# Two hybrid decoder layers on one core: the output projection's operand turned by VectorE and moved inside SBUF, and the SGU gate block ahead of the mLSTM gate block

## The chip, the core and the metric

The kernel runs on one core of a Trainium2 chip. Its engines run side by side, each with a queue of its own worked off in order: TensorE (PE, matmuls and transposes, results in PSUM), VectorE (DVE), ScalarE (ACT), GpSimd (POOL) and SyncE (SP, which here only issues transfers). They wait for one another by semaphores. The metric is the device time in microseconds (us) of the core; less is better.

## The reference

Two layers, 256 positions, width 2048, all in float32. One layer, cut to what matters here:

```
z = x @ w_in                       # attention q,k,v,gate; SGU u,v,gate; mLSTM q,k,v,o,gate
att = dilated_window_attention(...)                       # 512 columns
sgu = gelu(su) * (w_spatial @ layer_norm(gelu(sv)) + b)   # 512 columns
ml  = head_norm(mlstm(...) * sigmoid(mo))                 # 1024 columns, times a gain
mix = concat([att * silu(ag), sgu * silu(sg), ml * silu(mg)])
x   = layer_norm(alpha * x + mix @ w_out)
```

The matmul `mix @ w_out` needs `mix` with its columns on the partitions, that is, turned.

## The kernel before

**Blocks and chunks.** The projections run as 27 blocks of 512 output columns per layer. A block is 8 chunks of 256 input rows (`chunks`, L358). Float32 accuracy comes from splitting both operands into a high and a low part: a chunk is 2 row tiles x 2 position tiles x 3 products, 12 matmuls of 128x512. A chunk's weights are loaded by SyncE into a ring of four (`w_raw`, L324, 512 KB), ScalarE writes the high part (`w_hi`, L736) and VectorE the low part, the residue (`w_lo`, L1060). SyncE loads chunk c when the residue of chunk c - 4 is done; ScalarE overwrites a slot of `w_hi` when TensorE has used the chunk that was in it. All three write their work out by hand, in the order of the program; nothing is reordered.

**The end of a layer.** Blocks 21 and 22 are the second half of the mLSTM gate (`N_MG1`) and the SGU gate (`N_SG`); blocks 23 to 26 are the output projection (`N_OUT`). During block 21 TensorE also does the mLSTM value products, and VectorE the head outputs (`head_output`, L1419). During block 22 VectorE normalises the heads (L1462, `h_norm`), GpSimd multiplies by the head gain (L1732) and by the gate (L1737).

**The turned operand.** `mix` is [128 positions, 2, 2048]. TensorE turns it in 64 pieces, 32 per layer (`transposes`, L391, by a matmul with the identity), four pieces for a chunk of the output projection, into PSUM. ScalarE copies a chunk's high part out (L755) and VectorE the residue (L1084). The first block interleaves these with its chunks (`first_block`, L448), and `OUT_ORDER` puts the SGU columns, ready last, at the end:

```
                chunks(N_SG, Q_SG, 1, 0, 4)
                transposes(mix, CH, OUT_ORDER, 0, ((h_done, (l + 1) * MH), (mix_att, l + 1)))
                transposes(mix, CH, OUT_ORDER, 1)
                chunks(N_SG, Q_SG, 1, 4, CH)
                first_block(N_OUT, Q_OUT, mix, CH, OUT_ORDER, 2, ...
```

GpSimd also loads two rows broadcast over 128 partitions for the LayerNorm, 1 MB each: the gain into `z` (L1729) and the bias into `store` (L1741).

## Time and profile before

| | |
|---|---|
| median of 3 runs | 1271.35 us (1270.79 to 1271.76) |
| span of the profiled execution | 1269.9 us |
| TensorE busy | 1257.0 us (99%) |
| VectorE busy | 893.0 us (70%) |
| ScalarE busy | 705.4 us (56%) |
| GpSimd busy | 244.0 us (19%) |
| queue of SyncE's transfers, share of the 16 DMA engines | 60.6% |

The span runs from the first to the last instruction of one profiled execution; the median is of other executions, without a profile, and stands 1.45 us above it. Busy shares are means over the whole span. A matmul row's end is modelled, so starts of rows and the chain of work are the better clock on TensorE.

### The profile page before, as it was taken

The page shows a single profiled execution, that of the slowest core. Times are in us where ns is not written, and L with a number is a line of the kernel's source. Part 1 is how long each engine was busy: PE and PEld are TensorE (multiplying, and loading weights), DVE is VectorE, ACT ScalarE, POOL GpSimd, SP SyncE. Part 2 cuts the span into 40 slices and gives each one's busy share as a digit, 9 for nine tenths or more (in the row PEclk, how much of TensorE's full clock was granted, in tenths as well). Part 3 has the DMA queues.
Part 4 walks back from the last instruction along what each step waited for, and adds up shares of the span by engine and source line. Part 5 has one row for each costly group of instructions (what it writes and reads, how often), then busy time and mean ns, then how long its engine had stood idle before and what let it go on. Part 6 is the DMA issues. An engine that isn't in the chain of part 4 may idle for free.

```text
span 1269.9 us, 16388 instructions
## 1 busy us (share of the span) xinstructions
PE 1257.0 (99%) x6342; PEld 1040.2 (82%) x6342; DVE 893.0 (70%) x1229; ACT 705.4 (56%) x989; POOL 244.0 (19%) x268
## 2 busy tenths in 40 slices
PE   9999999999999999999999999999999999999996
PEld 8888888878888888888888788888888888888885
DVE  5686876876667655865785779768665776567656
ACT  5477476575555544444563775666755555345441
POOL 0321522522220000400003223334131200004000
PEclk9999999999999999999999999999999999999998
DMA  9968768765665555465657587678546556565562
GB/s 336 310 209 261 236 189 277 260 192 164 204 195 174 184 186 185 152 230 190 207 186 238 183 282 245 193 258 282 184 149 215 183 157 209 165 197 198 186 212 86
DMA packets 129277, 264.97 MB, mean 209 GB/s; under 512 B 8824, under 2 KB 8976, under 8 KB 128688
## 3 DMA queue, kind: packets, MB, share of 16 engines
q1 hardware_dynamic: 123712, 247.23, 60.6%
q0 software_dynamic: 3680, 13.28, 3.0%
q10 hardware_dynamic: 1808, 3.42, 0.7%
q8 instruction: 50, 0.82, 0.3%
q14 instruction: 27, 0.22, 0.0%
HBM read 258.61 MB, written 5.28 MB: 208 GB/s over the span
## 4 chain that ended last, share of the span: by engine, by line
PE 86%; ACT 4%; DVE 4%; POOL 3%; issue 2%; DVEq 0%; POOLq 0%; ACTq 0%
PE ps L373 79%; ACT arena L810 2%; DVE w_lo L1060 2%; ACT w_hi L736 2%; PE ps L444 1%; PE ps L671 1%; PE ps L391 1%; PE ps L639 1%; POOL arena L1684 1%; PE ps L533 0%; POOL arena L1680 0%; PE ps L518 0%; ACT arena L807 0%; PE ps L355 0%; DVE arena L1133 0%
## 5 line engine op out<-in xcount | busy, mean ns | idle before, releaser
L1060 DVE TENSOR_TENSOR w_lo<-w_raw,w_hi 128x1024 fp32r<-128x1024 f32 x408 | 527.1, 1305 | 326.4 <-ACT w_hi L736 324.5
L736 ACT ACTIVATE w_hi<-w_raw 128x1024 fp32r<-128x1024 f32 x408 | 427.3, 1058 | 388.9 <-PE ps L373 339.3
L373 PE MATMUL ps<-w_hi,xT_hi 128*128 128x512 f32 x1616 | 636.2, 394 | 0.7 <-DVE w_lo L1060 0.7
L373 PE MATMUL ps<-w_hi,xT_lo 128*128 128x512 f32 x1616 | 629.6, 390 | 0.0
L373 PE MATMUL ps<-w_lo,xT_hi 128*128 128x512 f32 x1616 | 629.0, 389 | 0.0
L373 PEld LDWEIGHTS ps<-w_hi,xT_hi 128*128 128x128 f32 x1616 | 303.4, 188 | 64.3 <-issue 1.3
L373 PEld LDWEIGHTS ps<-w_hi,xT_lo 128*128 128x128 f32 x1616 | 303.3, 188 | 64.0
L373 PEld LDWEIGHTS ps<-w_lo,xT_hi 128*128 128x128 f32 x1616 | 303.6, 188 | 61.4
L292 POOL TENSOR_TENSOR carried<-ident 1x1 f32<-1x1 f32 x30 | 19.6, 652 | 454.8 <-DVE arena L1416 178.7
L1217 DVE CUSTOM_DVE_ANT_0 mix<-xres,mix 128x1024 f32<-128x1024 f32 x64 | 89.0, 1390 | 1.1
L807 ACT ACTIVATE arena<-arena 32x256 f32<-32x256 f32 x128 | 53.2, 416 | 15.6 <-DVE arena L1137 14.0
L373 PE MATMUL ps<-ahead,xT_hi 128*128 128x512 f32 x160 | 49.8, 392 | 0.0
L1630 POOL TENSOR_TENSOR su<-z,sincos 128x128 f32<-128x128 f32 x24 | 23.6, 1005 | 122.0 <-ACT z L796 100.9
L1404 DVE SCALAR_TENSOR_TENSOR conv_y<-ps,cw,conv_y 128x255 f32<-128x255 f32 (+2 forms) x96 | 41.7, 476 | 1.1
L1060 DVE TENSOR_TENSOR ahead<-w_raw,ahead 128x1024 fp32r<-128x1024 f32 x23 | 27.5, 1223 | 15.1 <-ACT ahead L736 15.0
L736 ACT ACTIVATE ahead<-w_raw 128x1024 fp32r<-128x1024 f32 x23 | 23.8, 1056 | 22.8 <-DMA w_raw<-w_out_dram 7.2
L373 PEld LDWEIGHTS ps<-ahead,xT_hi 128*128 128x128 f32 x160 | 29.7, 188 | 5.9
L373 PE MATMUL ps<-ahead,xT_lo 128*128 128x512 f32 x80 | 31.2, 390 | 0.0
L810 ACT ACTIVATE arena<-arena 32x256 f32<-32x256 f32 x64 | 26.6, 416 | 7.3 <-DVE arena L1133 6.5
L825 ACT ACTIVATE arena<-arena 32x256 f32<-32x256 f32 x64 | 26.6, 415 | 6.8 <-DVE arena L1165 5.9
L967 ACT ACTIVATE arena<-conv_y 128x512 f32<-128x512 f32 x16 | 10.1, 633 | 32.7 <-DVE conv_y L1404 32.7
L1732 POOL TENSOR_TENSOR store<-store,hg 128x1024 f32<-128x1024 f32 x4 | 11.4, 2876 | 76.5 <-DVE store L1462 76.5
(244 smaller groups left out, 825.3 us busy)
## 6 DMA issues: line engine op xcount, KB each, us to landing
w_raw<-w_in_dram SPq DMA_DIRECT2D x367, 512.0 KB, 4.5
w_raw<-w_out_dram SPq DMA_DIRECT2D x64, 512.0 KB, 4.8
mix<-gate_w_dram SPq DMA_DIRECT2D x32, 512.0 KB, 5.6
xres<-x_dram ACTq DMA_DIRECT2D x4, 512.0 KB, 8.4
v_dram<-arena POOLq DMA_DIRECT2D x4, 512.0 KB, 6.3
z<-v_dram POOLq DMA_DIRECT2D x8, 256.0 KB, 5.6
z<-ln_g_dram POOLq DMA_DIRECT2D x2, 1024.0 KB, 7.7
store<-ln_b_dram POOLq DMA_DIRECT2D x2, 1024.0 KB, 7.9
```

Of the source, the lines that this page charges most:

```text
L292: nc.gpsimd.tensor_tensor(carried[0:1, at:at + 1], ident[0:1, 0:1], ident[0:1, 0:1], ALU.mult)
L373: mm = pe.matmul(ps[2 * s + t][:], a[:, order[c] * KC + k, t * P:(t + 1) * P], b[:, k], start=(c + k + i == 0), stop=(c == CH - 1 and k == ...
L391: tr = pe.transpose(ps[4 + u % 4][:, (k * TT + t) * P:(k * TT + t + 1) * P], src[:, t, at * P:(at + 1) * P], ident[:])
L444: mm = pe.matmul(ps[t][:], a[:, c * KC + k, t * P:(t + 1) * P], b[:, k], start=False, stop=(c == CH - 1 and k == KC - 1 and i == 2))
L736: A(hi_of(n, c), w_raw[:, c % RING], ACT.Copy).then_inc(w_hi_done, 1)
L807: mv_ = A(dst.rearrange("p m (r t u i) -> p u t (m r) i", r=RES, t=TT, u=4)[:, u], src.rearrange("p (t f q i) -> p f t q i", t=TT, f=4, i= ...
L810: mv_ = A(dst.rearrange("p m (t u s) -> p u t m s", t=TT, u=4)[:, u], src.rearrange("p (t m f s) -> p f t m s", t=TT, m=PAIRS, f=4)[:, f], ...
L825: e = A(pTC[f * 32:(f + 1) * 32, :, u * 32:(u + 1) * 32], zp[u * 32:(u + 1) * 32].rearrange("p (s f i) -> p f s i", s=SLOTS, f=4)[:, f], A ...
L1060: TTn(lo_of(n, c), w_raw[:, c % RING], hi_of(n, c).bitcast(F32), ALU.subtract).then_inc(w_lo_done, 1)
L1217: f = V.tensor_tensor_reduce(gate_junk, xres[:, tt, half * KH:(half + 1) * KH], gate_rows[buf], 1.0, 0.0, ALU.mult, ALU.add, gate_acc[:, t ...
L1404: f = STT(y, ps[4 + hf][:, t * SEQ:(t + 1) * SEQ - back], cw[:, m, j:j + 1], y, ALU.mult, ALU.add)
L1630: G.tensor_tensor(rope_a[:, :, :, c], v[:, :, :, c], trig(1), ALU.mult)
```

## The change

Per layer:

- Blocks 21 and 22 change places: the SGU gate is now block 21, the second half of the mLSTM gate block 22.
- TensorE's 32 transposes of `mix`, the functions `transposes` and `first_block` and the PSUM copies are gone. `mix` is handled in four parts of 512 columns: attention, SGU, first and second mLSTM half.
- VectorE turns a part in one instruction (`turn_mix`): each 32x32 square in itself, written to `mix_zT`. To reach a full turn the 32-row strips must change partitions: SyncE copies them in 16 transfers a part (`move`), each of 32 partitions x 2 x 128 numbers (32 KB), from `mix_zT` to `mix_T`.
- ScalarE and VectorE then write the high part and the residue of the operand from `mix_T` (`operand`), for the last part in two halves.
- SyncE issues the moves between weight loads: after the load of chunk 0 of block 22 (attention), of chunk 6 (first mLSTM half), of chunk 7 (SGU), and of chunk 7 of block 23 (second mLSTM half). Before each group it waits for the turn.
- GpSimd multiplies the SiLU of the first gate half by its gain early, and only the second half's heads by theirs after `h_norm`. VectorE does the products with the heads. Both halves of the SGU gate's SiLU are done by ScalarE from PSUM.
- The LayerNorm gain is loaded after the attention part's residue (its buffer `z` now holds that part), the bias after the product of the second mLSTM half.
- The output projection takes its chunks in plain order.

```diff
@@ -298,7 +314,17 @@
         @block.sync
         def _(sp):
             for l in range(DEPTH):
-                def load(w, n, col, order, gate=()):
+                def move(p):
+
+                    sp.wait_ge(mix_turned, l * PARTS + TURN_ORDER.index(p) + 1)
+                    src = mix_zT[p].rearrange("p (f t x) -> p f t x", f=4, t=TT)
+                    dst = mix_T[p].rearrange("p (t u x) -> p u t x", t=TT, u=4)
+                    for u in range(4):
+                        for f in range(4):
+                            sp.dma_start(dst[f * QUARTER:(f + 1) * QUARTER, u], src[u * QUARTER:(u + 1) * QUARTER, f]
+                                         ).then_inc(mix_moved[p], 16)
+
+                def load(w, n, col, order, gate=(), moves={}):
 
                     for c in range(CH):
...
+                        if c in moves:
+                            move(moves[c])
 
...
                     load(w_in, n, col * BW, plain)
+                load(w_in, N_MG1, (MG + 1) * BW, plain, moves={0: ATT, 6: ML_A, 7: SGU})
                 for i in range(D // BW):
-                    load(w_out, N_OUT + i, i * BW, OUT_ORDER)
+                    load(w_out, N_OUT + i, i * BW, plain, moves={7: ML_B} if i == 0 else {})
 
...
@@ -692,31 +695,28 @@
                     mm = pe.matmul(ps[o + 1][:, 0:MD + 1], scE[:, h, 2 * P:3 * P], vM[:, 1, h, :],
                                    start=False, stop=True)
                     mm.then_inc(mnum_ps, 1)
-                chunks(N_MG1, Q_MG1, 0, 5, CH)
-
-
-                chunks(N_SG, Q_SG, 1, 0, 4)
-                transposes(mix, CH, OUT_ORDER, 0, ((h_done, (l + 1) * MH), (mix_att, l + 1)))
-                transposes(mix, CH, OUT_ORDER, 1)
-                chunks(N_SG, Q_SG, 1, 4, CH)
-                first_block(N_OUT, Q_OUT, mix, CH, OUT_ORDER, 2, {
-                    2: ((h_done, (l + 1) * MH), (mix_ml, l + 1)),
-                    6: ((z_dve, taken_dve(l, Q_SG)),)})
+                chunks(N_SG, Q_SG, 0, 5, CH)
+
+                chunks(N_MG1, Q_MG1, 1, 0, CH)
+
+                for c in range(CH):
+                    pe.wait_ge(mixT_lo, step(l, c))
+                    chunks(N_OUT, Q_OUT, 0, c, c + 1)
                 for i in range(1, last_out):
-                    chunks(N_OUT + i, Q_OUT + i, i % 2, 0, CH, OUT_ORDER)
+                    chunks(N_OUT + i, Q_OUT + i, i % 2, 0, CH)
 
                 last = (N_OUT + last_out, Q_OUT + last_out, last_out % 2)
-                chunks(*last, 0, CH, OUT_ORDER, tiles=(1,), done=tile1_ps)
+                chunks(*last, 0, CH, tiles=(1,), done=tile1_ps)
                 if l == DEPTH - 1:
-                    chunks(*last, 0, CH, OUT_ORDER, tiles=(0,))
+                    chunks(*last, 0, CH, tiles=(0,))
                 else:
-                    chunks(*last, 0, 3, OUT_ORDER, tiles=(0,))
+                    chunks(*last, 0, 3, tiles=(0,))
                     unit(l + 1, 0)
                     unit(l + 1, 1)
...
-
-                    for u in range(u0, u1):
-                        if u >= c0:
-                            split(n, u, u + 1)
-                        act.wait_ge(xt_ps, mix_first(l) + u + 1)
-                        A(xT_hi[:, order[u] * KC:(order[u] + 1) * KC, :],
-                          ps[4 + u % 4][:].rearrange("p (k t) -> p k t", k=KC), ACT.Copy).then_inc(xt_hi, 1)
+                def operand(p, j=0, n=PART_TILES):
+
+                    act.wait_ge(mix_moved[p], (l + 1) * 16 * 16)
+                    act.wait_ge(w_used, used(l, N_MG1, 2 * p + 1))
+                    A(mix_target(xT_hi, p, j, n), mix_source(p, j, n), ACT.Copy).then_inc(mixT_hi, 1)
 
                 if l == 0:
                     for k in range(KC):
...
                 act.wait_ge(h_done, (l + 1) * MH)
                 A(rstd[:, 0], mv[:, :, :, 1], ACT.Sqrt, bias=eps[:]).then_inc(h_root, 1)
-                split(N_SG, 2, 4)
-                act.wait_ge(w_used, used(l, N_SG, -1))
-                A(mix[:, 0, 3 * BW:4 * BW], ps[0][:], ACT.Silu).then_inc(z_act, 1)
-                act.wait_ge(z_dve, taken_dve(l, Q_MG1))
-                A(mix[:, 1, 3 * BW:4 * BW], mix[:, 1, 3 * BW:4 * BW], ACT.Silu).then_inc(mg_silu, 1)
-                split(N_SG, 4, 8)
-                operand(N_OUT, RING, CH, OUT_ORDER, 0, 2)
-                split(N_OUT, 0, 4)
-                operand(N_OUT, RING, CH, OUT_ORDER, 2, 4)
+                split(N_MG1, 2, 4)
+                act.wait_ge(w_used, used(l, N_MG1, -1))
+                A(mix[:, 0, BW:2 * BW], ps[0][:], ACT.Silu)
+                A(mix[:, 1, BW:2 * BW], ps[1][:], ACT.Silu).then_inc(z_act, 1)
+                split(N_MG1, 4, 6)
+                operand(ATT)
+                split(N_MG1, 6, 8)
+                split(N_OUT, 0, 2)
+                operand(SGU)
+                split(N_OUT, 2, 4)
                 act.wait_ge(w_used, used(l, N_OUT, -1))
-                A(mix[:, 0, BW:2 * BW], ps[2][:], ACT.Silu)
-                A(mix[:, 1, BW:2 * BW], ps[3][:], ACT.Silu).then_inc(z_act, 1)
-                operand(N_OUT, RING, CH, OUT_ORDER, 4, CH)
+                A(mix[:, 0, 3 * BW:4 * BW], ps[2][:], ACT.Silu)
+                A(mix[:, 1, 3 * BW:4 * BW], ps[3][:], ACT.Silu).then_inc(z_act, 1)
+                operand(ML_A)
+                split(N_OUT, 4, 8)
+                operand(ML_B, 0, KC)
+                operand(ML_B, KC, KC)
                 for i in range(1, D // BW):
                     split(N_OUT + i, 0, 8)
 
...
-                        TTn(xT_lo[:, k, :], ps[4 + u % 4][:].rearrange("p (k t) -> p k t", k=KC),
-                            xT_hi[:, k, :].bitcast(F32), ALU.subtract).then_inc(xt_lo, 1)
+                def operand(p, at, j=0, n=PART_TILES):
+
+                    dve.wait_ge(mixT_hi, l * STEPS + at + 1)
+                    TTn(mix_target(xT_lo, p, j, n), mix_source(p, j, n), mix_target(xT_hi, p, j, n).bitcast(F32),
+                        ALU.subtract).then_inc(mixT_lo, 1)
+
+                def turn_mix(p):
+
+                    V.transpose(mix_zT[p].rearrange("p (f b s) -> p b f s", f=4, b=TT * PART_TILES),
+                                mix[:, :, p * BW:(p + 1) * BW]).then_inc(mix_turned, 1)
 
...
@@ -1443,33 +1443,49 @@
                         f = V.bn_aggr(mv[:, t, h, :], stats[:, t, h, :])
                     f.then_inc(h_done, 1)
 
-                split(N_MG1, 0, 4)
-                take(N_MG1, 1, vM[:, 1, 2:4, 0:MD])
-                split(N_MG1, 4, 5)
+                split(N_SG, 0, 4)
+                take(N_SG, 1, vM[:, 1, 2:4, 0:MD])
+                split(N_SG, 4, 5)
+                turn_mix(ATT)
 
                 dve.wait_ge(mo_sigmoid, l + 1)
                 for h in range(3):
-                    split(N_MG1, 5 + h, 6 + h)
+                    split(N_SG, 5 + h, 6 + h)
                     head_output(h)
-                split(N_SG, 0, 1)
+                split(N_MG1, 0, 1)
                 head_output(3)
-                split(N_SG, 1, 3)
+                split(N_MG1, 1, 3)
                 dve.wait_ge(h_root, l + 1)
                 own(V.reciprocal(rstd[:, 1], rstd[:, 0]))
-                for t in range(TT):
-                    for h in range(MH):
+                for h in range(MH):
+                    for t in range(TT):
                         v = store[:, 1 + h // 2, t, (h % 2) * MD:(h % 2 + 1) * MD]
                         f = TS(v, v, mv[:, t, h, 0:1], rstd[:, 1, t, h:h + 1], ALU.subtract, ALU.mult)
                 f.then_inc(h_norm, 1)
-                split(N_SG, 3, 4)
-                take(N_SG, 0, mix[:, 1, 3 * BW:4 * BW])
-                split(N_SG, 4, 8)
-                operand(N_OUT, RING, CH, OUT_ORDER, 0, 2)
-                split(N_OUT, 0, 4)
-                operand(N_OUT, RING, CH, OUT_ORDER, 2, 4)
+                dve.wait_ge(h_norm, l + 1)
+                dve.wait_ge(ml_gain, l + 1)
+                own(TTn(mix[:, :, 2 * BW:3 * BW], mix[:, :, 2 * BW:3 * BW], store[:, 1], ALU.mult))
+                turn_mix(ML_A)
+                split(N_MG1, 3, 4)
                 dve.wait_ge(z_act, taken_act(l, Q_SG))
                 TTn(mix[:, :, BW:2 * BW], mix[:, :, BW:2 * BW], su[:], ALU.mult).then_inc(z_dve, 1)
-                operand(N_OUT, RING, CH, OUT_ORDER, 4, CH)
+                dve.wait_ge(z_dve, taken_dve(l, Q_SG))
+                turn_mix(SGU)
+                split(N_MG1, 4, 6)
+                operand(ATT, 0)
+                split(N_MG1, 6, 8)
+                split(N_OUT, 0, 2)
+                operand(SGU, 1)
+                split(N_OUT, 2, 4)
+                dve.wait_ge(store_gain, l + 1)
+                dve.wait_ge(z_act, taken_act(l, Q_MG1))
+                TTn(mix[:, :, 3 * BW:4 * BW], mix[:, :, 3 * BW:4 * BW], store[:, 2], ALU.mult).then_inc(z_dve, 1)
+                dve.wait_ge(z_dve, taken_dve(l, Q_MG1))
+                turn_mix(ML_B)
+                operand(ML_A, 2)
+                split(N_OUT, 4, 8)
+                operand(ML_B, 3, 0, KC)
+                operand(ML_B, 4, KC, KC)
 
                 def residual(i, t):
...
-                pool.wait_ge(msc_done, (l + 1) * MH)
+                pool.wait_ge(mg_silu, l + 1)
+                for t in range(TT):
+                    v = mix[:, t, 2 * BW:3 * BW]
+                    f = G.tensor_tensor(v, v, hg[:, 0], ALU.mult)
+                f.then_inc(ml_gain, 1)
+
+                pool.wait_ge(h_norm, l + 1)
+                for t in range(TT):
+                    f = G.tensor_tensor(store[:, 2, t, :], store[:, 2, t, :], hg[:, 1], ALU.mult)
+                f.then_inc(store_gain, 1)
+                pool.wait_ge(mixT_lo, l * STEPS + 1)
                 carry_pool()
                 pool.dma_start(ln_gain, row(ln_g, 0, D)).then_inc(ln_gain_landed, 16)
-                pool.wait_ge(h_norm, l + 1)
-                for t in range(TT):
-                    f = G.tensor_tensor(store[:, 1:3, t, :], store[:, 1:3, t, :], hg[:], ALU.mult)
-                own(f)
-                pool.wait_ge(mg_silu, (l + 1) * 2)
-                for t in range(TT):
-                    v = mix[:, t, 2 * BW:4 * BW].rearrange("p (a c) -> p a c", a=2)
-                    f = G.tensor_tensor(v, v, store[:, 1:3, t, :], ALU.mult)
-                f.then_inc(mix_ml, 1)
-                pool.wait_ge(mix_ml, l + 1)
+                pool.wait_ge(z_dve, taken_dve(l, Q_MG1))
                 carry_pool()
                 pool.dma_start(ln_bias, row(ln_b, 0, D)).then_inc(ln_bias_landed, 16)
 
```

SyncE's queue in layer 0, from the last gate-weight loads of the attention part to the start of layer 1, before:

```order
L310 DMA mix<-gate_w_dram 128x1024 x2
L324 DMA w_raw<-w_in_dram 128x2x512 x92
L324 DMA w_raw<-w_out_dram 128x2x512 x32
L324 DMA w_raw<-w_in_dram 128x2x512 x20
L310 DMA mix<-gate_w_dram 128x1024 x2
```

and now:

```order
L350 DMA w_raw<-w_in_dram 128x2x512 x85
L324 DMA z<-arena 32x2x128 x16
L350 DMA w_raw<-w_in_dram 128x2x512 x6
L324 DMA arena<-arena 32x2x128 x16
L350 DMA w_raw<-w_in_dram 128x2x512
L324 DMA arena<-arena 32x2x128 x16
L350 DMA w_raw<-w_out_dram 128x2x512 x8
L324 DMA arena<-arena 32x2x128 x16
L350 DMA w_raw<-w_out_dram 128x2x512 x24
```

The row of 124 loads is cut in four places by 16 small transfers; one load stands alone between the second and the third group.

VectorE's queue from the second and third residue of block 22 on (L1060 is a weight residue, L1084 an operand residue before and a turn now, L1079 an operand residue now), before:

```order
L1060 TENSOR_TENSOR w_lo<-w_raw,w_hi 128x1024 x2
L1458 RECIPROCAL rstd<-rstd 128x8
L1462 TENSOR_SCALAR store<-store,mv,rstd 128x256 x8
L1060 TENSOR_TENSOR w_lo<-w_raw,w_hi 128x1024
L1095 COPY mix<-ps 128x512
L1060 TENSOR_TENSOR w_lo<-w_raw,w_hi 128x1024 x4
L1084 TENSOR_TENSOR xT_lo<-ps,xT_hi 128x512 x2
L1060 TENSOR_TENSOR w_lo<-w_raw,w_hi 128x1024 x4
```

and now:

```order
L1459 RECIPROCAL rstd<-rstd 128x8
L1463 TENSOR_SCALAR store<-store,mv,rstd 128x256 x8
L1467 TENSOR_TENSOR mix<-mix,store 128x2x512
L1084 STREAM_TRANSPOSE arena<-mix 128x8x4x32
L1060 TENSOR_TENSOR w_lo<-w_raw,w_hi 128x1024
L1471 TENSOR_TENSOR mix<-mix,su 128x2x512
L1084 STREAM_TRANSPOSE arena<-mix 128x8x4x32
L1060 TENSOR_TENSOR w_lo<-w_raw,w_hi 128x1024 x2
L1079 TENSOR_TENSOR xT_lo<-z,xT_hi 128x1024
L1060 TENSOR_TENSOR w_lo<-w_raw,w_hi 128x1024 x4
```

A product and a turn have come in front of the residue of chunk 3, and another pair in front of that of chunk 4.

## Rows read from the trace of the kernel before

**Rows 1.** The page, busy time: engine, busy us (share of span), instructions.
```profile
PE 1257.0 (99%) x6342; PEld 1040.2 (82%) x6342; DVE 893.0 (70%) x1229; ACT 705.4 (56%) x989; POOL 244.0 (19%) x268
```

**Rows 2.** List of waits, TensorE: total us, times, longest us.
```profile
PE ps L355 <- POOL ident L1567: 1.6, 1, 1.6
PE ps L373 <- DVE w_lo L1060: 0.7, 1, 0.7
```

**Rows 3.** Chain of waits in order of time: start us, us, what.
```profile
510.41 19.06 PE ps L373 x84
529.47 0.87 PE ps L391 x8
...
541.27 0.87 PE ps L391 x8
...
1158.16 0.87 PE ps L391 x8
```

**Rows 4.** Instructions by line: count, ns min/median/max, first and last start.
```profile
L1133 DVE STREAM_TRANSPOSE arena<-z x4: 1230/1238/1248, 244.9 to 895.8; 128x1024 f32<-128x1024 f32 x4
L1137 DVE STREAM_TRANSPOSE arena<-z x16: 1094/1132/1155, 63.5 to 806.4; 128x512 f32<-128x512 f32 x16
L1060 DVE TENSOR_TENSOR w_lo<-w_raw,w_hi x408: 1176/1225/3499, 15.5 to 1242.2; 128x1024 fp32r<-128x1024 f32 x136
L1084 DVE TENSOR_TENSOR xT_lo<-ps,xT_hi x16: 672/681/685, 535.7 to 1185.5; 128x512 fp32r<-128x512 f32 x16
L736 ACT ACTIVATE w_hi<-w_raw x408: 1037/1060/1112, 14.4 to 1241.2; 128x1024 fp32r<-128x1024 f32 x136
L755 ACT ACTIVATE xT_hi<-ps x16: 577/582/621, 530.5 to 1184.2; 128x512 fp32r<-128x512 f32 x16
```

**Rows 5.** Timeline of VectorE: start us, us, line, count, [idle before]; merged rows include gaps.
```profile
497.32 2.36 DVE L1060 TENSOR_TENSOR w_lo<-w_raw,w_hi 128x1024 fp32r<-128x1024 f32 x2 [2.83 <-ACT w_hi L736]
...
517.05 1.23 DVE L1060 TENSOR_TENSOR w_lo<-w_raw,w_hi 128x1024 fp32r<-128x1024 f32 x1 [1.49 <-ACT w_hi L736]
...
518.42 2.67 DVE L1462 TENSOR_SCALAR store<-store,mv,rstd 128x256 f32<-128x256 f32 x8
...
524.48 3.50 DVE L1060 TENSOR_TENSOR w_lo<-w_raw,w_hi 128x1024 fp32r<-128x1024 f32 x1 [1.65 <-ACT w_hi L736]
...
524.48 11.30 DVE L1060 TENSOR_TENSOR w_lo<-w_raw,w_hi 128x1024 fp32r<-128x1024 f32 x4 [1.65 <-ACT w_hi L736]
```

**Rows 6.** Timelines of GpSimd and ScalarE in block 22, same columns.
```profile
524.49 2.40 POOL L1732 TENSOR_TENSOR store<-store,hg 128x1024 f32<-128x1024 f32 x1
...
521.05 0.60 ACT L986 ACTIVATE mix<-ps 128x512 f32<-128x512 f32 x1
```

**Rows 7.** SyncE's issues: by line (ns min/median/max), and timeline (start us, us, count).
```profile
L324 SPq DMA_DIRECT2D w_raw<-w_out_dram x20: 367/368/368, 528.0 to 579.2; - x20
...
L320 SPq DMA_DIRECT2D mix<-x_t_dram x7: 358/469/537, 1.8 to 13.1; - x7
...
0.81 0.86 SPq L315 DMA_DIRECT2D w_raw<-w_in_dram  x2
...
528.01 0.37 SPq L324 DMA_DIRECT2D w_raw<-w_out_dram  x1
```

**Rows 8.** Transfers: issuing queue, count, KB each, median us from issue to landing.
```profile
w_raw<-w_in_dram SPq DMA_DIRECT2D x367, 512.0 KB, 4.5
w_raw<-w_out_dram SPq DMA_DIRECT2D x64, 512.0 KB, 4.8
...
store<-ln_b_dram POOLq DMA_DIRECT2D x2, 1024.0 KB, 7.9
out_dram<-xres SPq DMA_DIRECT2D x4, 512.0 KB, 2.7
```

**Rows 9.** Stretches at the end: us, busy by engine, granted clock, DMA share, GB/s.
```profile
1258.00:1260.00 2.00, 1.83 (x9) 1.18 (x7) 0.13 (x1) 0.00 (x0) 0.00 (x0) 1.00 0.13 51
...
1262.00:1264.00 2.00, 0.00 (x0) 0.00 (x0) 2.00 (x3) 0.00 (x0) 0.00 (x0) 0.70 0.00 0
```

72 lines of the change are left out of this document (30 added, 42 removed).

## The prediction, made before the changed kernel ran

> **What bounds the kernel now.** I read the busy table first: TensorE is busy 1257.0 us, 99% of the span of 1269.9 [rows 1]. The list of waits says the same from the other side: after the 1.6 us at the very start, the longest wait of a matmul on another engine is 0.7 us [rows 2]. So every microsecond taken from TensorE's instruction stream is a microsecond of the kernel, as long as nothing else arrives late; and each new late arrival is paid in full. Next I read the chain of work around the output projection of layer 0 [rows 3]. It is matmuls without a break: seven chunks in 19.06 us, so 2.72 us for a chunk (12 matmuls), then pieces of transposes between the chunks.
>
> That gives the clock face for the rest. Call the two gate blocks A (block 21) and B (block 22), and a block's chunks A0 to A7. From 510.41 on stand A5, A6, A7 and B0 to B3 [rows 3]; so B0 starts at 518.6, B3 at 526.8 and B4 at 529.5. Layer 1 shows the same picture 628.7 us later (the transposes of 529.47 are there at 1158.16 [rows 3]).
>
> **What is removed.** Eight transposes take 0.87 us of the chain [rows 3], 0.109 us each. There are 32 per layer, which makes 3.5 us, and 7.0 us in both layers. All of it is on the path. With no transposes, B4 to B7 would run from 529.5 to 540.4 and the first chunk of the output projection, O0, would start at 540.4.
>
> **What is added on VectorE, and when.** Per layer: four turns of 128x1024, two products of 128x1024, and residues of the operand in five instructions from SBUF instead of eight from PSUM. The nearest row for a turn is the one with whole runs, 1.24 us [rows 4]; the strided form took 1.13 for half the size, 2.26 for a full one [rows 4]. The new turn writes runs of 32, so I take 1.24 and keep 2.26 as the far end. A residue of 128x1024 takes 1.22, and a product of that size is priced the same [rows 4]. The operand's residues nearly cancel (eight of 0.68 [rows 4] against 4 x 1.22), so 4 x 1.24 + 2 x 1.22 = 7.4 us per layer are new. VectorE isn't the bound, so this sum doesn't matter; its place does.
>
> The attention turn stands in block A after A4's residue. VectorE does A4 and A5 there from 497.3 to 499.7 [rows 5], and TensorE reaches A5 only at 510.4: hidden, priced at nothing. If that cover were gone it would cost its 1.24 us.
>
> In block B it is tight. VectorE ends B2's residue at 518.2 and the eight normalising instructions at 521.1 [rows 5]. Before, B3's residue came next. Now a product and a turn come first: 521.1 + 1.22 + 1.24 = 523.6. GpSimd multiplies by the head gain from that same moment; in the trace its 128x1024 product takes 2.40 us [rows 6], and VectorE's residue that starts beside it takes 3.50 instead of 1.22 [rows 5], that is, it waits until GpSimd is through. The changed kernel has only 128x512 there, half of 2.40; so I add 1.2 us (0 at the good end): the turn ends at 524.75. B3 follows at 526, before 526.8. Then product, turn, B4: 526 + 1.22 + 1.24 + 1.22 = 529.7 against 529.5, a stall of 0.2 at most here. On the credit side four large GpSimd products, which now stretch four residues to 11.3 us [rows 5], are gone. The other edits there (the loop order of the normalising, a copy of 0.68 us off VectorE, a SiLU more on ScalarE in its place) stay under a microsecond on engines that then wait for TensorE; the two small gain products that GpSimd now does in the mLSTM part cost VectorE 1.2 us each at most, where a residue has some 6 us to spare. ScalarE has its SiLU output at 521.7, and 0.6 later the second [rows 6], in time for the second product.
>
> **What is added on SyncE, the term that decides.** Each part is carried by 16 transfers of 32 KB, all issued by SyncE, which also issues every weight load, in order. The moves stand behind the loads of B0 (attention), B6 (first mLSTM half), B7 (SGU) and O7 (second mLSTM half). What waits for them is the load written next: B1, B7, O0 and O8 (the next block's first). Issuing a load takes 0.367 us of the queue, and never less around the output projection [rows 7]; two issues in a row at the start took 0.86 us, 0.43 each, and seven issues in the crowded start took 0.47 in the median and up to 0.54 [rows 7]. No row shows a 32 KB copy inside SBUF being issued. I take 0.42, near the pitch of the two in a row; the ends are 0.37 (nothing between issues) and 0.54. Below the lower end I see no row, but rival 1 asks what it would bring.
>
> B1: held until about 499.8 + 16 x 0.42 = 506.5, lands 4.5 us later [rows 8], at 511; ScalarE can't take it before A5 is used, at 513.1. Hidden.
>
> B7: SyncE waits for the turn at 524.75, then 16 x 0.42 = 6.7 us: issued at 531.5, landed at 536.0, and with ScalarE's 1.06 and VectorE's 1.22 [rows 4] plus 0.1 between them ready at 538.4. TensorE wants it at 537.6: 0.8 late.
>
> O0: one load and 16 more issues, 7.1 us: issued at 538.6. In the kernel before it was issued at 528.0 [rows 7]. It lands after 4.8 us [rows 8] and is split 2.4 us later: 545.8. TensorE is free for it at 540.4. **A stall of 5.4 us** (with B7's part in it). The following loads go out at once behind it and don't stall again.
>
> Second mLSTM half: counted from O0's start, VectorE does O1, the SGU residue, O2 and O3, the product and the turn, six steps of about 1.2, so the turn ends at +7.2. The last of 16 issues starts at +13.5. For the landing I have 2.7 us (SBUF to DRAM, idle) as a lower end and 4.5 (a weight load) as an upper one [rows 8]; I take 3.4, between the two, since the bias row of the LayerNorm, 1 MB, is loaded beside it and takes 7.9 us [rows 8]. Then 0.58 + 0.68 [rows 4] for half a part: +18.2. TensorE wants it for O6 at 6 x 2.72 = +16.4: **a stall of 1.8 us.** The load of O8, issued at +13.9, is ready at +21.1, and TensorE wants it at 16.4 + 1.8 + 5.4 = +23.6: hidden.
>
> The GpSimd loads move too: the LayerNorm gain, 1 MB, is now fetched after the attention residue, about 533, beside the SGU moves, where before it was fetched in the mLSTM part. I price it inside the 4.8.
>
> **The sum.** Per layer -3.5 + 5.4 + 1.8 = +3.7; two layers +7.4. The profiled execution spans 1269.9 us, and the median of the runs is 1271.35, that is 1.45 above the span; the same 1.45 is kept: 1269.9 + 7.4 + 1.45 = 1278.8 us, 0.6% slower.
>
> **Weighed against the Trainium skill.** An issue costs SyncE at least 0.36 to 0.37 us whether the transfer has 256 or 512 KB [rows 7]. DMA: Bandwidth & Descriptors (Rules for kernel authors) says to coalesce many small transfers because under 64 KB one pays mostly overhead; that speaks against 128 transfers of 32 KB. The same page (Issuing engines are not separate DMA queues) says that the time on the issuing sequencer is usually small beside the transfer; if so, the pitch would hardly count and the full gain would show, 1264.3. By the trace it isn't small here. Its fit for one transfer (2.0 us plus bytes at 436 GB/s; Anatomy of one DMA), given for GpSimd's path, would make an estimate of 2.1 us for the landing of the last move instead of 3.4, and the sum 2.6 us smaller; no row here shows that.
>
> **Rivals.**
> 1. The queue holds nothing up; faster. The stalls shrink by 33 pitches and by 16 pitches. With 0.26 us or less the first is gone (5.4 - 33 x 0.16), the second too, and the whole 7.0 us show: 1264.3. Even balance is at 49 x (0.42 - p) = 3.7, so p = 0.345. Below that pitch the kernel is faster. For it: the issue row may hold work that grows with the load's 256 rows. Against: the first two loads, of half the size, took 0.43 each all the same [rows 7].
> 2. Gain and stall cancel. Pitch 0.37, no collision with GpSimd, a landing of 4.0: O0 stalls 5.4 - 1.65 - 1.2 - 0.8 = 1.8, the second half 1.8 - 0.8 - 0.7 = 0.3. Net -1.4 per layer: 1268.5, at the edge of no change; with only two of the three, about 1271.
> 3. The queue is worse than thought. Pitch 0.54 as under load: O0 stalls 5.4 + 4.0, the second half 1.8 + 1.9 + 1.1 with a landing of 4.5; net +10.7 per layer: 1292.8. The pieces of 512 bytes, and the 1 MB rows beside them, could do that.
> 4. The clock. TensorE's granted clock is 1.00 (2.4 GHz) while it works; its last matmul ends at about 1259.8, and over 1262 to 1264 the mean is 0.70 [rows 9], so the clock has fallen to the lower level (0.5, 1.2 GHz) some 3 us after the stop. A stall of 5.4 us is long enough for that. At half speed the first chunks of O take up to 2.7 us longer, of which the second stall hides 1.8, since its chain doesn't pass through TensorE: 0.9 per layer, 1280.6. It goes with the forecast and stays inside its width.
> 5. The turns are slow (2.26 us): two turns stand before B4, so up to 2 us more at O0 and 1 at the second half: +6, 1284.8.
>
> **How the numbers follow.** Forecast with 4 and 5 around it: 0.50. Rival 3: 0.15. Rival 2: 0.15. Rival 1, in full or between 1264 and 1268.8: 0.20. A measurement of this kernel can tell about 0.2%, 2.5 us, from no change. Slower by more: 0.50 + 0.15 = 0.65. Within: 0.15. Faster: 0.20. The range reaches from inside rival 1 to rival 3's end: 1266 to 1292.
>
> **What would show it.** In the profile of the changed kernel: (a) the 64 transposes of the mix are gone and each chunk of O0 to O7 follows the last without a gap of 0.44 us; (b) SyncE's queue shows four bursts of 16 issues per layer, each 6 to 9 us; (c) ScalarE waits on the DMA of w_out for O0, and TensorE on the residue of that chunk, about 5 us, in both layers; (d) a second, shorter wait of TensorE at O6, put down to the operand's residue; (e) no wait in block A. What would make it wrong: bursts under 5 us, or O0's load issued before 533. If TensorE waits already at B4, the turn or the collision with GpSimd was mis-sized and not the queue.

## The result, and the profile of the changed kernel

| | before | changed |
|---|---|---|
| median of four runs | 1271.55 us | 1301.0 us |
| profiled execution, its span | 1269.9 us | 1300.9 us |
| TensorE busy, share of the span | 1257.0 us, 99% | 1264.3 us, 97% |

The changed kernel takes 1.0229 of the time before (95% interval 1.0215 to 1.0244): 2.3% slower, 29.5 us. The prediction said slower, by 0.6%, 1278.8 us with a range of 1266 to 1292. The sign held; the time lies 9 us above the range.

The page's busy row of the changed kernel stands against [rows 1]; its waits of TensorE (total us, times, longest) stand against [rows 2], where the longest was 0.7 us behind the start.

```profile
PE 1264.3 (97%) x6278; PEld 1041.6 (80%) x6278; DVE 897.5 (69%) x1233; ACT 705.0 (54%) x983; POOL 236.0 (18%) x268
```

```profile
PE ps L402 <- DVE w_lo L1060: 20.5, 9, 5.0
PE ps L402 <- DVE xT_lo L1079: 4.2, 2, 2.2
PE ps L384 <- POOL ident L1583: 1.6, 1, 1.6
```

TensorE now waits for split weights (w_lo) and for the operand of the output projection (xT_lo). Its busy time has grown by 7.3 us although 7.0 us of transposes are gone: some of its matmuls ran slower.

SyncE's timeline of layer 0 (start us, length us, line, transfer, count) shows the four bursts of moves (L324) and the loads (L350) between them:

```profile
499.79 11.39 SPq L324 DMA_DIRECT2D z<-arena  x16
511.22 9.15 SPq L350 DMA_DIRECT2D w_raw<-w_in_dram  x6
525.37 10.18 SPq L324 DMA_DIRECT2D arena<-arena  x16
535.59 0.58 SPq L350 DMA_DIRECT2D w_raw<-w_in_dram  x1
536.22 10.49 SPq L324 DMA_DIRECT2D arena<-arena  x16
546.76 11.67 SPq L350 DMA_DIRECT2D w_raw<-w_out_dram  x8
560.48 10.45 SPq L324 DMA_DIRECT2D arena<-arena  x16
```

A burst takes 10.2 to 11.4 us, that is 0.64 to 0.71 us for an issue. B7's load goes out at 535.59, O0's at 546.76, where it was 528.01 before [rows 7]. ScalarE, which splits the weights first, waits for just these two, and already for B1's load, held up by the attention burst (its timeline, idle time before the row in brackets):

```profile
515.09 1.06 ACT L736 ACTIVATE w_hi<-w_raw 128x1024 fp32r<-128x1024 f32 x1 [4.77 <-DMA w_raw<-w_in_dram]
...
541.49 1.06 ACT L736 ACTIVATE w_hi<-w_raw 128x1024 fp32r<-128x1024 f32 x1 [13.54 <-DMA w_raw<-w_in_dram]
550.99 1.06 ACT L736 ACTIVATE w_hi<-w_raw 128x1024 fp32r<-128x1024 f32 x1 [8.45 <-DMA w_raw<-w_out_dram]
...
572.20 1.15 ACT L752 ACTIVATE xT_hi<-arena 128x512 fp32r<-128x512 f32 x2 [4.87 <-DMA arena<-arena]
```

And TensorE, in its own timeline:

```profile
527.64 0.50 PE L402 MATMUL ps<-w_hi,xT_hi 128*128 128x512 f32 x1 [0.84 <-DVE w_lo L1060]
...
543.86 0.79 PE L402 MATMUL ps<-w_hi,xT_hi 128*128 128x512 f32 x1 [4.25 <-DVE w_lo L1060]
...
553.46 0.76 PE L402 MATMUL ps<-w_hi,xT_hi 128*128 128x512 f32 x1 [4.11 <-DVE w_lo L1060]
...
573.60 0.59 PE L402 MATMUL ps<-w_hi,xT_hi 128*128 128x512 f32 x1 [1.99 <-DVE xT_lo L1079]
...
1197.16 0.76 PE L402 MATMUL ps<-w_hi,xT_hi 128*128 128x512 f32 x1 [5.01 <-DVE w_lo L1060]
...
1218.14 0.50 PE L402 MATMUL ps<-w_hi,xT_hi 128*128 128x512 f32 x1 [2.16 <-DVE xT_lo L1079]
```

These are the first matmuls of B3, B7, O0 and O6 in layer 0, and of O0 and O6 in layer 1. The stretches between them show the granted clock (columns: stretch, its length, TensorE's busy time and matmuls, clock, DMA share, GB/s):

```profile
540.00:543.80 3.80, 0.00 (x0) 0.92 0.51 158
543.80:549.20 5.40, 5.34 (x12) 0.50 0.32 79
...
553.40:557.00 3.60, 3.54 (x9) 0.53 0.79 278
557.00:570.00 13.00, 13.00 (x59) 1.00 0.76 226
...
573.60:577.00 3.40, 3.40 (x9) 0.54 0.99 348
```

After each of the three long waits of layer 0 TensorE works at the lower level (0.5, 1.2 GHz): the twelve matmuls of B7 take 5.3 us, where a chunk takes 2.72 at full clock [rows 3].

**The balance of a layer.** O0 starts at 553.46 and not at 540.4: 13.1 us. From O0 to O6 it takes 20.1 us in place of 16.3: 3.8. After O6 nine matmuls stand 0.43 apart and not 0.23: 1.8. Less 3.5 for the transposes, that is 15.2; the chain of work in layer 1 begins its end 14.9 us later than before (1124.18, 1109.24 before). In layer 1 O0 is late by 13.1 again (1197.16, where 540.4 + 628.7 + 14.9 is 1184.0), but from O0 to O6 it takes 21.0 us, 4.7 too many, behind a burst of 11.2 us, and after O6 seven slow matmuls cost 1.4: less 3.5, 15.7. Together that is 30.9; the spans differ by 31.0. The waits of 0.84 and 0.51 us before B3 and B4 add nothing: they lie before O0, inside its 13.1.

### The profile page after: what moved, and what is told of

Its sections match the earlier page's. It is cut to its first block, busy times and chain, and to the rows that moved or that the text cites. A ratio compares the mean times of both kernels' runs of the same rounds, so it can differ in the third digit from the quotient of the medians.

```text
span 1300.9 us, 16392 instructions
## 1 busy us (share of the span) xinstructions
PE 1264.3 (97%) x6278; PEld 1041.6 (80%) x6278; DVE 897.5 (69%) x1233; ACT 705.0 (54%) x983; POOL 236.0 (18%) x268
## 4 chain that ended last, share of the span: by engine, by line
PE 79%; SPq 6%; DVE 5%; ACT 3%; issue 2%; DMA 2%; POOL 2%; DVEq 0%; POOLq 0%; ACTq 0%
PE ps L402 73%; SPq L324 6%; DVE w_lo L1060 2%; PE ps L458 1%; ACT w_hi L736 1%; PE ps L674 1%; DMA w_raw<-w_out_dram 1%; DMA w_raw<-w_in_dram 1%; DVE arena L1084 1%; DVE mix L1217 1%; PE ps L642 1%; PE ps L536 0%; PE ps L521 0%; ACT arena L803 0%; ACT arena L806 0%
## 5 line engine op out<-in xcount | busy, mean ns | idle before, releaser
L1060 DVE TENSOR_TENSOR w_lo<-w_raw,w_hi 128x1024 fp32r<-128x1024 f32 x408 | 519.2, 1286 | 344.3 <-ACT w_hi L736 342.0
L1751 POOL TENSOR_TENSOR store<-store,hg 128x512 f32<-128x512 f32 x4 | 7.2, 1826 | 208.6 <-DVE store L1463 208.6
L1060 DVE TENSOR_TENSOR ahead<-w_raw,ahead 128x1024 fp32r<-128x1024 f32 x23 | 27.6, 1223 | 16.6 <-ACT ahead L736 16.6
```

What stands on the lines that cost most here:

```text
L1060: TTn(lo_of(n, c), w_raw[:, c % RING], hi_of(n, c).bitcast(F32), ALU.subtract).then_inc(w_lo_done, 1)
```

## Experiments

Chunk names are those of the prediction: A and B the last two gate blocks, O the first output block. "ML_A" and "ML_B" are the two mLSTM halves of the operand. Where an experiment's length matters, it stands against the kernel before on the same chip (1271.6 to 1272.0 us).

**1. What an issue costs by itself.** Behind the last stores of the kernel before, seven groups of eight transfers on SyncE with nothing else running.

```
+for i in range(8):                 # group 1, the change's own move
+    probe(pieces_of(dst, (i + 1) % 4, i), pieces_of(src, i % 4, i))
+landed()
+...                                # groups 2 to 7: other forms
```

> The kernel before, and behind its last stores seven groups of eight transfers that SyncE issues with nothing else running; each group waits until it has landed. They differ in form: (1) the change's own move, 32 partitions x 2 runs of 512 bytes, SBUF to SBUF, 32 KB; (2) 32 partitions x one run of 1 KB, SBUF to SBUF, 32 KB; (3) 128 partitions x 256 bytes, SBUF to SBUF, 32 KB; (4) 128 partitions x 2 KB, SBUF to SBUF, 256 KB; (5) form 1 from DRAM; (6) form 1 to DRAM; (7) 128 partitions x 2 KB from DRAM, 256 KB. In the changed kernel an issue of form 1 takes 0.597 us and the next starts 0.64 us after it. Theory A (the price is the form's own, paid on the issuing engine): group 1 shows 0.60 each and a pitch of 0.64 here too, with an idle machine, and one of the other forms falls to the 0.37 of the weight loads: 2 if it is the two runs, 5 and 6 if it is that both sides are in SBUF, 3 or 4 if it is the 32 partitions. Theory B (the price is the load of the DMA engines, which the weight loads keep 60% busy): group 1 falls to 0.37 to 0.43 and all seven forms look alike. The time of the whole kernel grows by 56 issues and seven landings, about 50 us, and is of no interest.

One row per form (duration of the issue in ns, min/median/max): groups 1, 2, 3 and 4, then 5, 6 and 7.

```profile
L352 SPq DMA_DIRECT2D mix<-xres x8: 596/596/763, 1270.7 to 1275.4; - x8
...
L352 SPq DMA_DIRECT2D mix<-xres x8: 562/590/592, 1277.3 to 1281.7; - x8
...
L352 SPq DMA_DIRECT2D mix<-xres x8: 519/601/603, 1283.6 to 1288.0; - x8
...
L352 SPq DMA_DIRECT2D mix<-xres x8: 465/606/617, 1289.9 to 1294.3; - x8
...
L352 SPq DMA_DIRECT2D mix<-w_in_dram x8: 348/427/427, 1297.0 to 1300.3; - x8
...
L352 SPq DMA_DIRECT2D v_dram<-xres x8: 310/427/429, 1302.1 to 1305.3; - x8
...
L352 SPq DMA_DIRECT2D mix<-w_in_dram x8: 351/432/667, 1306.9 to 1310.1; - x8
```

Theory A holds in one of its forms: a transfer with both ends in SBUF takes 0.60 us to issue, one with an end in DRAM 0.43, and the number of rows, the runs and the size (32 or 256 KB) make no difference. Nothing else was being transferred, so it isn't the load of other transfers. A group's eight starts lie 0.63 to 0.67 and 0.46 to 0.47 us apart.

**2. A quarter of the moves.** The other three quarters of the operand's squares are not moved; that work is left out.

```
-                        for f in range(4):
+                        for f in (u,):
```

> The changed kernel with 4 of the 16 moves of each part, those that stay within their 32 partitions (the other three quarters of the operand's blocks are not moved: that work is left out). Theory A (SyncE's queue): a burst takes 4 x 0.64 = 2.6 us. The first mLSTM turn ends at 525.35 as now, B7's load goes out at 527.9, the SGU turn is there at 528.75, O0's load goes out at 531.3, lands at 535.5 and is split at 538, before the 540.4 at which TensorE wants it; the second mLSTM half is ready 7.2 + 2.6 + 1.9 + 1.3 = 13 us after O0's start and wanted after 16.4. No wait is left but those before B3 and B4 (1.3 to 2.2 us per layer), and the clock stays at 1.00: 1264.3 + 2.6 to 4.4 = 1267 to 1268.7 us. Rival B (VectorE, the swapped blocks or the turns are what costs, not the issues): the time stays within a few us of 1301. Rival C (the transfers' own bytes and landings, not the issuing): the last landing sets the operand, which moves by under 1 us: above 1290.

1265.84 us, 0.9958 of before (0.9941 to 0.9974), 1 us under the expectation because the waits before B3 and B4 went too: with a short attention burst B1's load isn't late, and the first mLSTM turn ends at 523.16 (525.35 in the changed kernel). O0's load went out at 530.37, and no wait of TensorE above 0.7 us is left but the one at the start. So turns, products, swapped blocks and the edits on ScalarE and GpSimd cost the critical path next to nothing: of the 7.0 us of the transposes, 5.9 show in the medians (1271.74 to 1265.84) and 7.3 in the two profiled spans. It can't tell issues from bytes, since both fell to a quarter; the next run does.

**3. The same bytes in twice the issues.**

```
+                            for t in range(TT):
+                                sp.dma_start(dst[f * QUARTER:(f + 1) * QUARTER, u, t],
+                                             src[u * QUARTER:(u + 1) * QUARTER, f, t]) ...
```

> The changed kernel with each move cut in two (16 KB, one run of 512 bytes per partition): 32 issues in a part, the same bytes and the same pieces. Theory A1 (an issue costs its 0.64 us whatever is in it): bursts of 20.5 us; B1 comes 5 us late, O0's load 21 us later than in the changed kernel, the second mLSTM half 10 us later: about 35 us more per layer, some 1370 us. Theory A2 (an issue is paid by its pieces, of which it now has half): the pitch falls to 0.32 us, bursts stay near 10.2 us, and the time stays at 1301 within 5 us. Between them: a pitch of 0.42 (0.37 for the issue and little for the pieces), bursts of 13.4 us, about 1313 us. Rival C (the DMA engines are held by pieces, not the queue by issues): 1301, whatever the pitch.

1380.89 us (1.086, 1.084 to 1.088). The bursts are 20.2 us for 32 issues, again 0.63 each, with half the bytes in each:

```profile
534.69 20.22 SPq L325 DMA_DIRECT2D arena<-arena  x32
554.96 0.58 SPq L351 DMA_DIRECT2D w_raw<-w_in_dram  x1
555.58 20.13 SPq L325 DMA_DIRECT2D arena<-arena  x32
```

Theory A1: the issue is what is paid, not its bytes. The time is 11 us above the 1370 expected. The attention burst of 21.0 us now reaches TensorE as well: it waits 5.7 us for B1, which the expectation had named as a lateness of 5 us.

**4. The halves of the loss.** "late" moves only the second mLSTM half in full, "mid" only the first half and the SGU part; the other parts make 4 of 16 moves, and the rest of their work is left out.

```
-                        for f in range(4):
+                        for f in range(4) if p in FULL else (u,):
```

> Only the second mLSTM half is moved in full (16 issues); of the other three parts 4 of 16 moves are made, and the rest of them is left out. With 4 moves in every part the time was 1265.8 us and TensorE waited nowhere here; there the burst of this part began at 547.0, and O6 started at about 556.4. Queue theory: 16 issues at 0.64 us end at 557.3, the last lands 1.9 to 2.7 us later, ScalarE and VectorE take 1.3: O6 starts at 560.9, 4.5 us late, with up to 1 us more for the clock after the wait. Per layer 4.5 to 5.5: 1275 to 1277 us, with a wait on the operand at O6 alone and none on w_in or w_out at B7 and O0. Rival (this part is hidden, only the loads' lateness counts): 1266.

> The opposite of the run before: the first mLSTM half and the SGU part are moved in full (16 issues each), of the attention part and the second mLSTM half 4 of 16 moves are made and the rest is left out. Queue theory: B7's load goes out at 535.6 and O0's at 546.8 as in the changed kernel, O0 starts at 553.5 in place of 540.4, and the clock loses some 1.5 us more in O0: 13.1 + 1.5 = 14.6 us per layer over the 1265.8 of the run with 4 moves in each part, that is 1295 us (1293 to 1297). No wait on the operand at O6. If the attention part's burst mattered too (ScalarE waited 4.8 us for B1's load behind it), the sum of this run's and the last run's excess falls short of the changed kernel's 35 us by more than 3 us; if the two waits overlap, it goes over it.

"late" took 1278.19 us (1.0051, 1.0036 to 1.0066), 12.3 over the run with a quarter of the moves and 1 over the expectation; O6 started at 560.62 (560.9 expected), and six matmuls a layer ran at the lower clock. "mid" took 1292.17 us (1.0165, 1.0148 to 1.0182), 26.3 over it, 3 short of the expectation: O0 started at 552.73. Together 38.7, and the changed kernel lies 35.2 above the same run. The two halves overlap by 3.5 us. The attention part made four moves in both, so these sums leave it nothing to add; its effect in the changed kernel is taken up below.

**5. The queue alone, in the kernel before.** Idle copies that nobody waits for, in the kernel before with its transposes and its order.

```
+                        if (n, c) in ((N_SG, 0), (N_SG, 6), (N_SG, 7), (N_OUT, 7)):
+                            burst()        # 16 copies of 16 KB, ident -> unused
```

> The kernel before, unchanged in all its work (transposes, order of the blocks, VectorE's instructions), with idle bursts on SyncE's queue: 16 copies inside SBUF (32 partitions x 512 bytes, into a tile that nobody reads) behind the loads of chunks 0, 6 and 7 of the last gate block and behind the eighth chunk of the output projection, where the changed kernel has its moves. They wait for no other engine. Queue theory: B6's load goes out near 522.9, its burst holds B7's load until 533.1, the next burst O0's load until 543.9 (528.0 in the kernel before); it lands 4.8 us later and is split 2.4 us after that, at 551.1. TensorE wants it at 543.9: 7.2 us late, with 1.5 to 2 us more at the lower clock. The burst behind O7 is hidden, since nobody waits for these copies and O8's load has the time. 8.7 to 9.2 us per layer: 1289 to 1290 us (1286 to 1292), with waits on the loads alone. Rival (the loss in the changed kernel comes from VectorE's turns, the swapped blocks or the operand's landing, not from the queue): 1271 to 1273.

1289.01 us (1.0133, 1.0117 to 1.0148), as expected. SyncE's queue and TensorE's one new wait in layer 0:

```profile
530.82 10.93 SPq L308 DMA_DIRECT2D unused<-ident  x16
541.79 11.32 SPq L335 DMA_DIRECT2D w_raw<-w_out_dram  x8
```

```profile
548.68 0.77 PE L387 MATMUL ps<-w_hi,xT_hi 128*128 128x512 f32 x1 [6.21 <-DVE w_lo L1074]
```

Copies that do nothing for the result cost 17 us. Next only their source was changed, to DRAM, of which an issue takes 0.43 us:

```
-unused[...], ident[u * 32:u * 32 + 32, :]
+unused[...], w_in[l, u * 32:u * 32 + 32, f * P:(f + 1) * P]
```

> The kernel before with the same idle bursts as in the run with copies inside SBUF (16 issues of 16 KB behind chunks 0, 6 and 7 of the last gate block and the eighth chunk of the output projection), only that the source is DRAM. Alone on the queue an issue of this kind took 0.427 us and came every 0.47, against 0.60 and 0.65 inside SBUF. Pitch theory: the bursts shrink from 10.0 to 7.5 us; B7's load goes out at 527.1 (529.6 with SBUF copies), the next burst starts about 528.5 and ends at 536, O0's load goes out at 536 and not at 541.8, and TensorE, which waited 6.2 us at O0, waits 0.4 or not at all: 1272 to 1276 us. Rival (it is the number of transfers or their load on the DMA engines that delays, whatever the issue takes): within 3 us of the 1289 of that run. If the landings of these DRAM copies are slow, the second burst, which waits for the first, starts up to 2 us later: 1276 to 1280.

```profile
527.17 7.27 SPq L308 DMA_DIRECT2D unused<-w_in_dram  x16
534.49 13.97 SPq L335 DMA_DIRECT2D w_raw<-w_out_dram  x8
```

```profile
544.33 0.76 PE L387 MATMUL ps<-w_hi,xT_hi 128*128 128x512 f32 x1 [2.50 <-DVE w_lo L1074]
```

1278.85 us (1.0054, 1.0037 to 1.0071). 10 of the 17 us are gone by 0.17 us less per issue. It is 3 us above the pitch theory's range all the same: O0's load went out 1.5 us sooner than I expected, but it landed after 7.4 us (4.4 in the run with SBUF copies). GpSimd fetched the LayerNorm bias, 1 MB, from 534.34 on, just beside it; in the run with SBUF copies it did so at 535.47, 6 us ahead of the load. This collision I had not in the sum. That it is the cause is likely and not shown, since the copies themselves also read DRAM here.

**6. Another queue.** All moves issued by GpSimd.

```
+                move(pool, l, ATT)
                 ...                     # head gain, second half
+                move(pool, l, ML_A)
+                move(pool, l, SGU)
                 ...                     # LayerNorm gain
+                move(pool, l, ML_B)
```

> The changed kernel with all 64 moves of a layer issued by GpSimd; SyncE issues loads only. Theory A (SyncE's queue held up the loads): O0's load goes out at about 528 as in the kernel before, B7 and O0 are not late. What is left depends on GpSimd's own pitch q, which no row shows for this form (its issue of the LayerNorm gain took 0.60 us). GpSimd is through with the head gain at 526.5, then 32 issues for the first mLSTM half and the SGU part: at q = 0.6 the SGU part has landed at 548 where O2 wants it at 545.8, so a wait of 3 to 5 us at O2; the second mLSTM half, 16 issues after a turn at O0 + 7.2, comes as late as now, 2 to 4 us. Net of the 3.5 us for the transposes: 1271 to 1283 us, waits on the operand (O2, O6) and none on w_in or w_out. With q near 1.0 the SGU part lands at 560, 14 us late, and the time is above 1295, again by waits on the operand alone. Rival B (the loads are late for lack of DMA bandwidth or by contention with the pieces): ScalarE still waits over 5 us for the DMA of w_in and w_out around B7 and O0.

1294.8 us (1.0185, 1.0169 to 1.02). GpSimd's issues took 0.54 us; SyncE's load of O0 went out at 528.95. TensorE still waited 4.4 us, on w_lo, in O2, and 5.1 us, on the operand, in O6 (4.0 and 6.4 in layer 1):

```profile
550.02 0.77 PE L407 MATMUL ps<-w_hi,xT_hi 128*128 128x512 f32 x1 [4.42 <-DVE w_lo L1067]
...
568.98 0.80 PE L407 MATMUL ps<-w_hi,xT_hi 128*128 128x512 f32 x1 [5.14 <-DVE xT_lo L1086]
```

```profile
546.42 1.06 ACT L759 ACTIVATE xT_hi<-arena 128x1024 fp32r<-128x1024 f32 x1 [9.33 <-DMA arena<-arena]
547.38 1.99 ACT L741 ACTIVATE w_hi<-w_raw 128x1024 fp32r<-128x1024 f32 x2
```

The weight was there. ScalarE, which works in order, stood at the SGU operand, whose 16 moves GpSimd had issued behind those of ML_A, and the split of O2's weights stood behind it. Another queue moves the waiting; it doesn't take it away. So the turn of ML_B ended only at 553.4, its 16 moves were issued by 563.0, and O6 was late too. The expectation had both places right, and its upper end for q = 0.6 was 12 us too low: I had not counted what stands behind the operand on ScalarE, the second gate among it.

**7. Cut in among the loads, and shared.** "spread" keeps all on SyncE, "shared" divides them.

```
spread: moves={0: ATT 0-5, 1: ATT 6-10, 2: ATT 11-15, 7: ML_A 0-3}   (last gate block)
        moves={0..3: SGU 4 each, 3..5: ML_A 4 each, 7: ML_B 16}      (first output block)
shared: GpSimd: ATT 16, ML_A 16, ML_B 6;  SyncE: O0..O2: SGU 6, 5, 5, O7: ML_B 10
```

> The changed kernel with the same 64 moves per layer, all still on SyncE, but cut in among the loads: attention 6, 5, 5 behind the loads of B0, B1, B2; first mLSTM half 4 behind B7 and 4 each behind O3, O4, O5; SGU 4 each behind O0 to O3; the second mLSTM half 16 behind O7 as now. Queue theory: it is not the number of issues but what stands behind them. O0's load goes out at about 528 to 530 and TensorE doesn't wait at B7 or O0; only the second mLSTM half stays late, 4.2 us at O6 and up to 1 us of clock: 1274 to 1276 us. Rival (the sum of all issues or of all pieces is what costs): near 1301. If ScalarE, which takes the SGU operand and then the splits of O2 and O3 in order, gets that operand later than 537, O2 is late by the same amount: up to 3 us more per layer.

> The same 64 moves on two queues: GpSimd issues the attention part, the first mLSTM half and 6 of the second half; SyncE issues the SGU part cut in behind the loads of O0, O1, O2 (6, 5, 5) and 10 of the second mLSTM half behind O7. GpSimd's pitch was 0.53 us and its landing 4.0 us. The LayerNorm gain's load comes after the last of GpSimd's moves. Queue theory: no load is late; first mLSTM half landed by 538 (wanted at 544); second half: turn at 547.6, SyncE's ten issues end at 554.0 and land at 555.9, GpSimd's six end at 552 and land at 556; O6 at 557.2 in place of 556.8. So the whole gain of the transposes but 0.4 to 1 us per layer: 1266 to 1268 us, 0.3 to 0.4% faster than the kernel before. If landings behind loads in flight take 5 to 6 us as they did for the first moves of that burst, 2 us more per layer: up to 1271. Rival (two queues stand in each other's way, or GpSimd's issues are held up by VectorE): above 1275.

1286.82 us (1.0117, 1.01 to 1.0135) and 1285.54 us (1.0109, 1.0094 to 1.0124): both better than the changed kernel by 14 to 15 us, both missed by 11 us and more. O0 was in time in both. In "spread" ScalarE got the SGU operand only at 546.56, and TensorE waited 4.1 us in O2 and 3.3 in O6. In "shared" ScalarE got the SGU operand at 543.45 (wanted at 537), so its SiLU of the second gate came at 547.51 and the turn of ML_B at 551.3, not at 547.6; the whole chain moved with it. That is 3.7 us; O6 came 8 us later than expected (565.25, not 557.2). The moves of that part took up to 6.7 us to land, with both LayerNorm rows fetched from 555.78 on; experiment 8 tries this out in another order. My expectations had followed the queue and not ScalarE's order.

**8. The chain put in order.** "tuned": SGU moves 8 and 8 on two queues at once, the SGU operand ahead of O1's split, the second gate ahead of O3's. "rows_late": besides, the two LayerNorm rows are fetched only after the last piece of the operand. "tuned2": besides, ML_B 8 and 8, SyncE's eight ahead of O7's load.

```
 rows_late:
-                pool.wait_ge(mixT_lo, l * STEPS + 1)
+                pool.wait_ge(mixT_lo, l * STEPS + STEPS)
                 carry_pool()
                 pool.dma_start(ln_gain, row(ln_g, 0, D)).then_inc(ln_gain_landed, 16)
```

> The changed kernel's work in full, with its moves on two queues and three steps reordered. GpSimd issues the attention part, 5 moves of the first mLSTM half, 8 of the SGU part, the other 11 of the first half, 6 of the second; SyncE issues 8 of the SGU part behind O0's load and 10 of the second half behind O7's. ScalarE and VectorE take the SGU operand before the split of O1 (it was behind it), and the gate of the second mLSTM half, its product and its turn before the split of O3 (they were behind it). The two runs before this one showed why: the SGU operand came late in ScalarE's stream, so the gate and the turn behind it came at 551.3 and not at 547.6. Queue theory: SGU moves end at 534.7 on SyncE and 534 on GpSimd, landed by 538; O0 at 540.4 without a wait; gate at 541.8, turn of the second half ends at 544.5 to 545.3; SyncE's ten moves issued by 551.7, GpSimd's six landed by 553.6; the operand is ready at 555 to 556, and TensorE wants it at 556.8. No wait: 1264.3, and up to 1 us per layer where a landing behind the loads takes 5 us: 1264 to 1267 us, 0.4 to 0.6% faster than the kernel before. Rival (a landing behind the loads of O6 and O7 and the LayerNorm rows costs over 6 us, or another link of ScalarE's chain takes the place of the one removed): a wait at O6 or O2 of 2 to 5 us per layer and 1269 to 1276 us.

> The tuned order of the last run with one change: GpSimd fetches the LayerNorm gain and bias (1 MB each) only when VectorE has the last piece of the operand, where before they were issued at 550.3 and 551.4, beside the last moves of the second mLSTM half. In the last run the turn came at 545.7 as planned, SyncE's ten moves were issued from 547.3 to 553.7, but its last five took 5.2 to 6.9 us to land; alone on the queue such a move took 1.9. Theory L1 (the two rows of 1 MB lengthen the landing): it falls to 2 to 3.5 us, the operand arrives 3 us sooner, O6 at 558.5 in place of 561.4: 3 to 4 us less per layer with the clock, 1272 to 1274 us. Theory L2 (the three weight loads issued from 541.9 to 546.9 lie ahead of the moves, the rows don't matter): 1279 to 1281 as before. Theory L3 (the issuing alone sets the end): the same as L2, since the last issue still starts at 553.1.

> As the run before, and two changes more: the second mLSTM half is shared 8 and 8 (10 and 6 before), and SyncE issues its eight behind O6's load, ahead of O7's, at the turn's end (545.7) and not at 547.3. Queue theory: SyncE's eight end at 550.9, GpSimd's eight at 551.2 (0.53 us each from 546.9); with a landing of 3 to 4 us they are there at 555, the operand's first half is ready at 556.3, and TensorE wants it at 556.8; O7's load goes out at 551, lands at 556 and is split at 558.4, wanted at 559.5. No wait, or under 0.5 us: 1264 to 1267 us, 0.4 to 0.6% faster than the kernel before. If landings stay at 5 to 7 us whatever is beside them, O6 comes at 558.5 to 560: 1269 to 1273 us.

"tuned" took 1279.87 us (1.0064, 1.0052 to 1.0077). The turn came at 545.8, about as planned, but a wait of 4.6 and 5.2 us at O6 was left, as its rival said, and the time is 4 us above that rival's range too: with GpSimd fetching both rows from 550.28 on, SyncE's last five moves took 5.2 to 6.9 us to land (min/median/max of "DMA to landing"; the first pair is "tuned", the second "rows_late"):

```profile
L321 SPq DMA_DIRECT2D arena<-arena x5: 596/596/601, 550.5 to 553.1; - x5
...
DMA to landing us min/median/max: 5.2/6.7/6.9
```

```profile
L321 SPq DMA_DIRECT2D arena<-arena x6: 596/597/600, 550.1 to 553.3; - x6
...
DMA to landing us min/median/max: 1.8/2.6/3.6
```

"rows_late" took **1265.41 us, 0.9951 of before (0.9936 to 0.9967)**: with all the work and all 64 moves it beats both kernels. Theory L1 was right in kind and too small in size (1272 to 1274 expected): both waits at O6 went (none is left in layer 0, 0.6 us in layer 1), and the slow matmuls behind them as well. "tuned2" was meant to be better still and took 1271.88 (0.9995, 0.9987 to 1.0004). O7's load now stood behind eight moves, and ScalarE splits O7 before it takes the last operand:

```profile
556.66 1.06 ACT L741 ACTIVATE w_hi<-w_raw 128x1024 fp32r<-128x1024 f32 x1 [5.86 <-DMA w_raw<-w_out_dram]
557.62 1.13 ACT L759 ACTIVATE xT_hi<-arena 128x512 fp32r<-128x512 f32 x2
```

The moves had landed by about 553.4; the operand waited for a weight that it doesn't need.

**9. Were the rows a cause in the changed kernel too?** Only the edit of "rows_late", on the changed kernel.

> The changed kernel with one change: the LayerNorm gain and bias (1 MB each) are fetched only when VectorE has the last piece of the operand. In the changed kernel the gain was issued at 534.5 and the bias at 559.4; B7's load, issued at 535.6, took 5.9 us to land. Theory Q (SyncE's issuing sets nearly all): B7's and O0's loads go out when they did, B7 lands 1.4 us sooner (4.5), and the second mLSTM half, whose last issue starts at 570.3, arrives as before, since its last moves already landed in 1.8 us: 1.4 us less per layer, 1297 to 1300 us. Theory L (the rows' bandwidth is a main cause here too, as in the tuned order): 1285 to 1292.

1299.03 us (1.0212, 1.0197 to 1.0228): theory Q. B7's load landed in 3.9 us (5.9 before), so B7 started 2.4 us sooner and ran at the full clock, and TensorE then waited 4.1 us longer for O0, which came only 0.8 us sooner:

```profile
541.48 0.50 PE L402 MATMUL ps<-w_hi,xT_hi 128*128 128x512 f32 x1 [2.23 <-DVE w_lo L1060]
552.69 0.77 PE L402 MATMUL ps<-w_hi,xT_hi 128*128 128x512 f32 x1 [8.16 <-DVE w_lo L1060]
```

In both layers together 18 matmuls ran at the lower clock in this trace, and 53 in the changed kernel's; that is 35 x 0.2 = 7 us less, of which 2.0 show in the medians and 4.3 in the two profiled spans. The clock lost in B7 is free, because O0 waits for its load anyway; the clock lost behind O6 is paid.

## Why the prediction came out low

1. **Bound by TensorE's stream, each late arrival paid in full**: held for the last late arrival of each chain, O0's load and O6's operand. B7's lateness wasn't paid besides, since O0 waits in any case (run 9). The waits of the changed kernel and their removal in runs 2 and 8 account for the time.
2. **Transposes, -3.5 us per layer**: held (7.3 us less span in run 2).
3. **Turns 1.24 and products 1.22 us**: 1.246 and 1.21 to 1.23 us. The turn was predicted to end at 524.75 and ended at 525.35, and that this fits is luck. The 1.2 us added for GpSimd fell on B3's residue (2.32 us), not on the product (1.23) or the turn (1.25): with a short attention burst, in run 2, the turn ends at 523.16, and that trace runs 0.5 us ahead (B0's load at 498.10, not 498.63), so at 523.7 on this clock face, as in the sum without the 1.2. In its place came B1's late load, 1.7 us (item 9). Waits before B3 and B4 came to 0.84 and 0.51 us against "0.2 at most". The prediction took a wait at B4 as the sign that the turn or GpSimd was mis-sized and not the queue; that sign misleads here, because the waits are gone in run 2 with the turns as they are.
4. **The pitch of an issue, taken as 0.42 us with ends at 0.37 and 0.54**: this is the step that failed. It measured 0.64, and bursts took 10.2 to 11.4 us where 6 to 9 were predicted. The nearest rows [rows 7] all had an end in DRAM, and so does 0.43 in run 1; the sentence "No row shows a 32 KB copy inside SBUF being issued" was the warning, and the upper end was still taken from rows of the other kind. By the prediction's own formulas the rest follows: O0's stall 5.4 + 33 x 0.22 = 12.7 us (13.1 measured), the second half's 1.8 + 16 x 0.22 = 5.3. The upper end was also the mildest of its kind: in the same crowded start of the kernel before, loads between those seven issues took 0.60 and 0.63 us.

```profile
3.19 0.63 SPq L324 DMA_DIRECT2D w_raw<-w_in_dram  x1
...
4.41 0.60 SPq L324 DMA_DIRECT2D w_raw<-w_in_dram  x1
```

5. **Landing of a move, 3.4 us**: the last of the burst took 1.8 us, so 5.3 falls to 3.7 (3.8 measured). On an idle machine run 1 measured 1.9; beside rows of 1 MB the same moves took 5.2 to 6.9 (run 8). The Trainium skill's fit (DMA: Bandwidth & Descriptors, Anatomy of one DMA), given for GpSimd's path, had made an estimate of 2.1 us: SyncE's free queue in run 1 agrees (1.9), the moves beside the rows of 1 MB don't (5.2 to 6.9).
6. **Issuing beside landing**: a burst is 16 x 0.64 = 10.2 us of issuing against a landing of 1.9, and doubling the issues cost 80 us. The Trainium skill (DMA: Bandwidth & Descriptors) says under Issuing engines are not separate DMA queues that the time on the issuing engine is usually small beside the transfer, which doesn't hold for this burst (10.2 us against 1.9), and under Rules for kernel authors that small transfers should be coalesced, which the 80 us for twice the issues bear out.
7. **The clock**, "up to 0.9 us per layer": TensorE fell to the lower level as rival 4 said, after waits of 2.0 to 5.0 us. Only the stretch behind O6, 1.8 us in layer 0 and 1.4 in layer 1, was paid. In B7 a later arrival hid it (run 9); in O0 by the trace too, since ScalarE takes O6's operand at 572.20 after 4.87 us of waiting for the moves. So nearly twice the estimate, for another reason than given: the prediction charged O0's stretch and not O6's.
8. **Sum**: -3.5 + 12.7 + 3.7 + 1.8 = 14.7 per layer, 29.4 for both, against 29.5 measured. The terms are not known that well: the traces give 14.9 for layer 0 and 16.0 for layer 1, so the fit to 0.1 us is luck. Rival 3 had the mechanism and a pitch of 0.54, and with it the range ended at 1292.
9. **Attention part hidden**: TensorE waited neither in block A nor for B1. But the burst took 11.4 and not 6.7 us, so ScalarE waited 4.77 us for B1's load, and VectorE began B2's residue at 518.75 and not at 517.05 [rows 5]. The normalising, the first mLSTM turn and the two bursts behind it came 1.7 us later, and B3 and B4 had their waits. In "mid", with four moves in the attention part, O0's load went out 1.7 us sooner (545.05), but O0 started only 0.7 us sooner (552.73), because the load took 5.2 us to land and not 4.2. It is the same failed term, the pitch, once more.

Not tried: the swap of the two gate blocks by itself. Run 2 only shows that the swap together with all the rest but three quarters of the moves costs next to nothing.

## What to carry to other kernels

Price a burst of small transfers by the queue that issues it: count the issues, multiply by the issue time of that very form (inside SBUF it was 1.4 times that with an end in DRAM here), and charge the product to the next load in the same queue. Then follow each late operand through the in-order engine that takes it, since what stands behind it there is late too: both of my repairs that followed only the queue missed by over 10 us. And a large transfer that nobody needs yet belongs behind the small ones that somebody waits for; moving two of them was worth 14 us in "tuned", where the moves landed beside them, and 2 us in the changed kernel, where the queue was the limit.

## What was not expected of the hardware

- On SyncE with nothing else running, the issue time depended on where the ends are and not on rows, runs or size: 0.60 us for SBUF to SBUF, 0.43 with one end in DRAM, for 32 and 256 KB. Spaced-out loads took 0.37 [rows 7], loads right behind others 0.43 to 0.59, two in the crowded start 0.60 and 0.63, and the longest in the kernel before 1.13, so in the running kernel the place of the ends isn't all.
- On GpSimd's queue the same issue took 0.54 us. In run 6 the move landed after 4.0 us in the median, against 1.9 on SyncE's in the changed kernel, but that doesn't show a slower queue: a burst on SyncE holds up the loads (the DMA engines were 18% busy over that of the first mLSTM half), and one on GpSimd runs beside them (69% over the same part). In "shared" GpSimd's last six moves landed in 1.8 to 2.1 us.
- The length of a wait alone doesn't tell whether TensorE's clock falls. In "tuned2" it stood at the lower level behind a wait of 2.3 us in layer 0, and stayed at the upper one behind a wait of 3.1 us at the same place of layer 1 (stretch, length, TensorE's busy time and matmuls, clock, DMA share, GB/s). What decides stays open.

```profile
559.60:563.00 3.40, 3.37 (x9) 0.56 0.64 207
...
1189.90:1193.00 3.10, 3.10 (x14) 1.00 0.77 241
```
